# Expert blocks of a routed layer: two weight panels split whole into high and low parts, six pair places, and the gate limit moved into a product

## The reference, cut to what matters

```python
SWIGLU_LIMIT, SWIGLU_ALPHA, EXPERT_BLOCK, D_FF_3 = 7.0, 1.702, 128, 1024

def clamped_swiglu_expert(xb, w_gu, b_gu, w_dn, b_dn):      # xb: (128, 1024)
    gu = xb @ w_gu + b_gu                                   # w_gu: (1024, 2048)
    gate = jnp.minimum(gu[:, :D_FF_3], SWIGLU_LIMIT)
    up = jnp.clip(gu[:, D_FF_3:], -SWIGLU_LIMIT, SWIGLU_LIMIT)
    glu = gate * jax.nn.sigmoid(SWIGLU_ALPHA * gate)
    return ((up + 1.0) * glu) @ w_dn + b_dn                 # w_dn: (1024, 1024)

xb = hf[row_tok].reshape(NB, EXPERT_BLOCK, D)
yb = lax.map(lambda a: clamped_swiglu_expert(a[0], w_gate_up[a[1]], ...), (xb, blk_e))
```

## Time and profile before

| what | value |
|---|---|
| median of 3 runs | 3327.51 us (3325.28 to 3328.65) |
| the profiled execution | 3326.17 us, span 3324.3 us, mean granted clock 0.961 |
| TensorE busy in the span | 3106.9 us (93%) |
| VectorE busy | 1850.6 us (56%) |
| ScalarE busy | 1596.8 us (48%) |
| GpSimd busy | 738.3 us (22%) |
| DMA traffic | 694.23 MB, mean 209 GB/s |

### The profile page before, as it was taken

How to read it: one execution, slowest core, us unless ns; L and a number is a source line. 1 busy time by engine, 2 the same in 40 slices (tenths; PEclk the granted TensorE clock), 3 DMA queues, 4 the chain that set the end, 5 groups by cost and what they waited for, 6 DMA issues and landing times. The chain is left out here.

```text
span 3324.3 us, 39326 instructions
## 1 busy us (share of the span) xinstructions
PE 3106.9 (93%) x14030; PEld 2418.4 (73%) x14030; DVE 1850.6 (56%) x2260; ACT 1596.8 (48%) x2142; POOL 738.3 (22%) x381
## 2 busy tenths in 40 slices
PE   7986999998999999989998985999999999999997
PEld 6754678877877787768887774777777777777753
DVE  3257433344467404440034346888888888888764
ACT  4333434433566423242233224766766676666652
POOL 3400144442523343334442510000000000000020
PEclk9987999998999999999999977999999999999998
DMA  3243322222222132212225407999999999999971
GB/s 148 102 167 112 127 76 101 101 95 83 77 76 76 54 112 76 102 51 101 100 103 198 177 10 311 403 408 412 405 407 411 407 407 411 411 402 411 411 265 48
DMA packets 65737, 694.23 MB, mean 209 GB/s; under 512 B 6928, under 2 KB 7312, under 8 KB 25584
## 3 DMA queue, kind: packets, MB, share of 16 engines
q1 hardware_dynamic: 54480, 650.57, 49.6%
q0 software_dynamic: 7056, 25.69, 2.0%
q10 hardware_dynamic: 4112, 16.78, 1.2%
HBM read 654.74 MB, written 38.27 MB: 208 GB/s over the span
## 5 line engine op out<-in xcount | busy, mean ns | idle before, releaser
L142 POOL TENSOR_TENSOR ring_low<-ring,mix_ring_high 128x1024 fp32r<-128x1024 f32 x120 | 292.7, 2473 | 451.9 <-ACT mix_ring_high L137 451.9
L213 PE MATMUL psum<-mix_high,mix_ring_high 128*128 128x512 f32 x864 | 344.1, 398 | 13.1 <-DVE h_low L518 8.6
L215 PE MATMUL psum<-mix_high,ring_low 128*128 128x512 f32 x864 | 338.1, 391 | 0.0
L213 PE MATMUL psum<-ex_high,ex_rows_high 128*128 128x512 f32 x768 | 315.8, 411 | 7.1 <-DVE ring_low L2852 7.1
L215 PE MATMUL psum<-ex_high,ex_rows_low 128*128 128x512 f32 x768 | 300.4, 391 | 0.0
L214 PE MATMUL psum<-h_low,mix_ring_high 128*128 128x512 f32 x736 | 287.7, 391 | 0.0
L142 POOL TENSOR_TENSOR ring_low<-ring,ff_ring_high 128x1024 fp32r<-128x1024 f32 x72 | 174.9, 2463 | 417.0 <-ACT ff_ring_high L137 226.5
L2683 POOL CAST ex_index<-table 128x1 uint32 x32 | 5.9, 184 | 1069.2 <-PE psum L2701 1069.2
L2852 DVE TENSOR_TENSOR ring_low<-ring,ex_high 128x2048 fp32r<-128x2048 f32 x96 | 214.2, 2287 | 40.5 <-ACT ex_high L2794 40.5
L2852 DVE TENSOR_TENSOR ex_more_low<-ex_more,ex_high_in_x 128x2048 fp32r<-128x2048 f32 x96 | 219.5, 2287 | 20.4 <-ACT ex_high_in_x L2794 20.4
L2750 PE MATMUL psum<-ex_more,ex_act_t 128*128 128x512 f32 x512 | 224.9, 592 | 0.0
(11 more groups left out here) (586 smaller groups left out, 6915.2 us busy)
## 6 DMA issues: line engine op xcount, KB each, us to landing
ex_more<-moe_w SPq DMA_DIRECT2D x128, 2048.0 KB, 9.3
ring<-wstream SPq DMA_DIRECT2D x87, 2048.0 KB, 8.3
ring<-moe_w SPq DMA_DIRECT2D x64, 2048.0 KB, 11.2
ex_bias_up<-moe_b SPq DMA_DIRECT2D x32, 1024.0 KB, 11.2
y_rows<-ex_y SPq DMA_DIRECT2D x33, 512.0 KB, 11.2
y_rows<-mx_zero ACTq DMA_DIRECT2D x1, 16384.0 KB, 50.9
x<-xt SPq DMA_DIRECT2D x8, 256.0 KB, 5.4
rel<-rel_bias SPq DMA_DIRECT2D x1, 2048.0 KB, 9.5
```

The costliest lines, as they stand in the source:

```text
L142: e.tensor_tensor(low, full, high.bitcast(F32), ALU.subtract).then_inc(self.low_ready, 1)
L213: pe.matmul(out, a[0], b[0], start=start, stop=False)
L215: return pe.matmul(out, a[1], b[0], start=False, stop=stop)
```

## The change

- All 24 quarters are split, 12 pairs. PIECES ends with (4,2), (4,3), (5,2), (5,3). The float32 product of line 2750, `ex_act_t`, `take_act` and the semaphores `dn_done`, `a_ready` and `limited` go. TensorE ends a block with four more quarters, behind a wait for the second `low_act`.
- The ring of high quarters has 12 places; the two new ones lie in the tile h. `held_before` says which quarter must be used up before a place is written: the one 12 earlier.
- `take_gate(0)`, `take_up(0)`, `take_gate(1)` stand before pairs 6, 8 and 10; `sigmoid(0)` ahead of copy 16; `take_y` stays ahead of copy 8.
- `act_high` and `act_low` have all 8 steps; `high_act` and `low_act` run once for each half. On VectorE the tail is `low_act(0)`, `take_up(1)`, `low_rows(0)`, `low_act(1)`, `low_rows(1)`.
- `take_gate` is the bias addition alone. The limit is taken as the minimum of the silu with its value at 7 (SILU_LIMIT), in the product with up; the factor 1/1.702 moves to the copy of y.
- SP loads panels 4 and 5 after their quarter 3.

```diff
+SILU_LIMIT = SW_ALPHA * SW_LIMIT / (1.0 + float(np.exp(-SW_ALPHA * SW_LIMIT)))
...
-    RING = 10
-    PIECES = tuple((s, c) for s in range(4) for c in range(PARTS)) + tuple((s, c) for s in (4, 5) for c in range(2))
+    PAIRS = 6
+    RING = 2 * PAIRS
+    PIECES = tuple((s, c) for s in range(4) for c in range(PARTS)) + ((4, 0), (4, 1), (5, 0), (5, 1), (4, 2), (4, 3), (5, 2), (5, 3))
...
-    act_at, dve_at = (8, 14), (10, 14, 18)
+    act_at, dve_at = (8, 16), (12, 16, 20)
...
+        high_in_h = nc.alloc_sbuf_tensor_at("ex_high_in_h", [P, 2, PART], F32R, offset=g.h_at)
...
+        def held_before(n):
+
+            if n >= RING:
+                return NQ + n - RING
+            return n + RING if n + RING < NQ else n
...
-                        if s < 4:
-                            sp.wait_ge(used, b * NQ + place[s, PARTS - 1] + 1)
-                        else:
-                            sp.wait_ge(dn_done, b * 2 + s - 3)
+                        sp.wait_ge(used, b * NQ + place[s, PARTS - 1] + 1)
...
-                    pe.wait_ge(a_low, b + 1)
+                    pe.wait_ge(a_low, b * 2 + 1)
...
-                    pe.wait_ge(a_ready, b + 1)
+                    pe.wait_ge(a_low, b * 2 + 2)
                     for s in (4, 5):
-                        for k in range(4, KT):
-                            mm = pe.matmul(psum[:, s + 2, :], act_t[:, k - 4, :], weights(s, k), start=False, stop=k == KT - 1)
-                        mm.then_inc(dn_done, 1)
+                        for c in range(2, PARTS):
+                            quarter(b, s, c, psum[:, s + 2, :], act_high, act_low)
...
-                        act.activation(y[:, 512 * s:512 * s + 512], psum[:, 6 + s, :], ACT.Copy).then_inc(y_done, 1)
+                        act.wait_ge(used, b * NQ + place[4 + s, PARTS - 1] + 1)
+                        act.activation(y[:, 512 * s:512 * s + 512], psum[:, 6 + s, :], ACT.Copy, scale=1.0 / SW_ALPHA).then_inc(y_done, 1)
...
-                        act.wait_ge(used, b * NQ + n + 1 + NQ - RING)
+                        act.wait_ge(used, b * NQ + held_before(n) + 1)
...
-                    high_act(b)
+                    high_act(b, 0)
                     sigmoid(b, 1)
                     act.wait_ge(x_turned, b * 2 + 3)
                     high_rows(0)
-                    take_act(b)
+                    high_act(b, 1)
...
-                    dve.wait_ge(taken, b * 4 + 2 * c + 5)
-                    dve.tensor_scalar(gate[:, :], gate[:, :], SW_LIMIT, None, ALU.min).then_inc(limited, 1)
...
-                    dve.scalar_tensor_tensor(act_rows[:, c, :], up[:, :], 1.0 / SW_ALPHA, sig[:, :], ALU.mult, ALU.mult).then_inc(h_done, 1)
+                    dve.scalar_tensor_tensor(act_rows[:, c, :], sig[:, :], SILU_LIMIT, up[:, :], ALU.min, ALU.mult).then_inc(h_done, 1)
...
-                    low_act(b)
+                    low_act(b, 0)
                     take_up(b, 1)
-                    for c in range(2):
-                        low_rows(b * 2 + 2 + c, c)
+                    low_rows(b * 2 + 2, 0)
+                    low_act(b, 1)
+                    low_rows(b * 2 + 3, 1)
```

More of the change, by code:

```diff
@@ L2603, in expert_stage @@
         high, bias_up = r.high, r.bias_up
-        high_in_x = nc.alloc_sbuf_tensor_at("ex_high_in_x", [P, RING - 6, PART], F32R, offset=g.x_at)
+        high_in_x = nc.alloc_sbuf_tensor_at("ex_high_in_x", [P, 4, PART], F32R, offset=g.x_at)
+        high_in_h = nc.alloc_sbuf_tensor_at("ex_high_in_h", [P, 2, PART], F32R, offset=g.h_at)
         rows_high, _ = on_line(nc, own, "ex_rows_high", [P, DT, P], F32R)
         rows_low = sb("rows_low", [P, DT, P], F32R)
-        act_high, act_low, act_t = sb("act_high", [P, 4, P], F32R), sb("act_low", [P, 4, P], F32R), sb("act_t", [P, 4, P])
+        act_high, act_low = sb("act_high", [P, KT, P], F32R), sb("act_low", [P, KT, P], F32R)
         part_of = lambda c: slice(c * PART, (c + 1) * PART)
@@ L2611, in expert_stage @@
         weights = lambda s, k: piece(s)[:, k * PANEL:(k + 1) * PANEL]
+        def held_before(n):
+            if n >= RING:
+                return NQ + n - RING
+            return n + RING if n + RING < NQ else n
         def slots(n, count):
             n %= RING
-            at = high[:, n:n + count, :] if n < 6 else high_in_x[:, n - 6:n - 6 + count, :]
+            tile, n = (high, n) if n < 6 else (high_in_x, n - 6) if n < 10 else (high_in_h, n - 10)
+            at = tile[:, n:n + count, :]
             return at.rearrange("p a f -> p (a f)")
@@ L2622, in expert_stage @@
         y = sb("y", [P, D])
-        used, high_ready, low_ready, dn_done = (sem(n) for n in ("used", "high_ready", "low_ready", "dn_done"))
+        used, high_ready, low_ready = (sem(n) for n in ("used", "high_ready", "low_ready"))
         x_turned, x_high, x_low, up_in = (sem(n) for n in ("x_turned", "x_high", "x_low", "up_in"))
-        taken, limited, sig_ready, product, h_done, h_turned, a_high, a_low, a_ready, y_done, y_out = (sem(n) for n in (
-            "taken", "limited", "sig_ready", "product", "h_done", "h_turned", "a_high", "a_low", "a_ready", "y_done", "y_out"))
+        taken, sig_ready, product, h_done, h_turned, a_high, a_low, y_done, y_out = (sem(n) for n in (
+            "taken", "sig_ready", "product", "h_done", "h_turned", "a_high", "a_low", "y_done", "y_out"))
         passed, table_set = (sem(n) for n in ("passed", "table_set"))
@@ L2696, in _ @@
                 pe.sem_inc(used, NQ)
-                pe.sem_inc(dn_done, 2)
                 def turn_rows(c):
@@ L2759, in high_rows, with high_act @@
                         .then_inc(x_high, 1)
[L2761 to L2767, removed]
+                def high_act(b, c):
+                    act.wait_ge(h_turned, b * 2 + c + 1)
+                    act.activation(act_high[:, 4 * c:4 * c + 4, :].rearrange("p k s -> p (k s)"), psum[:, 4, :], ACT.Copy).then_inc(a_high, 1)
                 def take_y(b):
@@ L2771, in take_y @@
                     for s in range(2):
-                        act.wait_ge(dn_done, b * 2 + s + 1)
-                        act.activation(y[:, 512 * s:512 * s + 512], psum[:, 6 + s, :], ACT.Copy).then_inc(y_done, 1)
+                        act.wait_ge(used, b * NQ + place[4 + s, PARTS - 1] + 1)
+                        act.activation(y[:, 512 * s:512 * s + 512], psum[:, 6 + s, :], ACT.Copy, scale=1.0 / SW_ALPHA).then_inc(y_done, 1)
                 def sigmoid(b, c):
-                    act.wait_ge(limited, b * 2 + c + 1)
+                    act.wait_ge(taken, b * 4 + 2 * c + 5)
                     act.wait_ge(h_done, b * 2 + c + 2)
@@ L2813, in low_rows, with low_act @@
                         .then_inc(x_low, 1)
[L2815 to L2818, removed]
+                def low_act(b, c):
+                    part = slice(4 * c, 4 * c + 4)
+                    dve.wait_ge(a_high, b * 2 + c + 1)
+                    dve.tensor_tensor(act_low[:, part, :].rearrange("p k s -> p (k s)"), psum[:, 4, :],
+                                      act_high[:, part, :].rearrange("p k s -> p (k s)").bitcast(F32), ALU.subtract)\
                         .then_inc(a_low, 1)
@@ L3224, in build @@
         g.sums, g.sums_at = placed(nc, ctx, "sums", [P, 3, S], F32)
+        g.h_at = -(-nc.sbuf_base // 32) * 32
         h, g.h_low = with_low(nc, ctx, "h", [P, DT, S])
```

## The result

| kernel | median (runs) | ratio to before, 95% interval |
|---|---|---|
| before | 3328.08 us | |
| changed | 3380.69 us (3379.75 to 3382.17) | 1.0158 (1.0146 to 1.0170) |

The change costs 52.6 us; 3351 us, +23, was forecast, in a range of 3340 to 3370, and the time lies above it. The profiled execution of the changed kernel took 3379.75 us (span 3377.9 us).

The account below looks back on a forecast made before the run. TensorE was taken as the bound at 35.96 us a block; after the change a loop through three engines, 36.68 us. Later `low_act(0)` (+26.4) less 2.5 won back gave +23.9 us: 3351 us, range 3340 to 3370.

Parts of the forecast that it names:

- What bounds the kernel before: Expert stage: TensorE, busy 300 of 300 us, sets the 35.96 us block; the DMA queue is close behind.
- Part 1: TensorE: split products replace the plain float32 product, saving 1.42 us a block; TensorE alone would give 34.54 us.
- Parts 2 and 3: VectorE gets 3.49 us more before `low_act(0)`; the loop through VectorE, TensorE and ScalarE goes from 33.19 to 36.68 us a block.
- the restart of TensorE: Between `low_act(0)` and quarter (4,0): 0.06 us after the subtraction's 0.68, together 0.74 us of the loop.
- the piece from (4,0) to `turn_act(1)`: TensorE's part of the three-engine loop, taken as 2.86 us in each block.
- rival (c): TensorE's idle 2.1 us a block drops its clock: +1.4 to +2.86 us a block, 3395 to 3440 us; 6%.
- Rival (a): The three-engine loop is shorter than reckoned, so TensorE or the DMA queue binds: about 3302 us, between 3281 and 3325; 9%.
- (b): The DMA queue holds the block at 35.96 us if the loop does not: no change, 3322 to 3333 us; 4%.
- (d): A supply wait besides, copy 9 or panel s5 late: +0.2 to +0.5 us a block, 3358 to 3368 us; 6%.
- the margin at pair 4: ScalarE's copy 9 ends at 3.1 us, VectorE's pair 4 wants it at 3.4: 0.3 us to spare.

Follow-up runs that it names:

- the kernel with the tail moved: Changed kernel with `low_act(0)`, `take_up(1)` and `low_rows(0)` put before pair 11 on VectorE instead of behind it: 3283.45 us, ratio 0.9869.
- The filled kernel: Changed kernel with 7 more matmuls, product overwritten, between `turn_rows(0)` and TensorE's wait for `low_act(0)`: 3352.91 us, ratio 1.0070.
- the kernel with the small bias load: Changed kernel with `low_act(0)`, `take_up(1)`, `low_rows(0)` before pair 11, and the bias load cut to 64 of 2048 columns: 3282.41 us, ratio 0.9865.

## Why the prediction was wrong

- **What bounds the kernel before: right.** VectorE's 0.92 us taken away there changes nothing, and TensorE's saving shows in full once no loop is in its way.
- **Part 1, TensorE at 34.54 us: right,** 34.54 measured in the kernel with the tail moved.
- **Parts 2 and 3, the loop at 36.68 us: right,** 36.73 in all blocks at full clock. The filled kernel, in which the clock stays up, has 3352.9 us against the forecast 3351. The only piece off by more than 0.02 us is the restart of TensorE, 0.82 for 0.74.
- **Where it failed: the sum took the piece from (4,0) to `turn_act(1)` at full clock in every block, 2.86 us, and the clock's falls at nothing.** In 17 of 31 blocks that piece took about 4.4 us, 27 us more in all. This is rival (c), which was given 6% and left out of the range. Its place and mechanism were right (TensorE's idle time before (4,0), then that piece at the lower clock) and its price per fall too (1.59 us, forecast 1.4 to 2.86). Its reach was not: I priced it as in every block or in none, 3395 to 3440, and the measured time lies between the forecast and that. The evidence that I weighed it by was one row, 2.66 us idle before 1140.16 with the clock at 1.00. One such gap shows that the clock can stay up after it, not that it will: in the changed kernel the same gap of 1.97 us, 31 times, had both outcomes. A fall in every second block was a case of its own, 3351 + 16 x 1.59 = 3376, and the range should have held it; the measured time is 4 us above that, of which 1.6 are the seventeenth fall and 1.5 the loop's.
- The Trainium skill, "TensorE: Matmul & The Clock Gate" (HAM oscillation), describes a loop in which a wait for a DMA, longer than the wait here, brought the clock down in every single pass. The changed kernel agrees that a wait in a loop can bring the clock down again and again, but not in every pass: 17 falls in 31 spacings.
- **Rival (a) did not come, and its floor was wrong too.** I took the best slice of the kernel before, 421 GB/s, as what the queue can do, so 34.8 us. The kernel with the moved tail carries 425 GB/s at 34.54 us and is not held by it: a rate seen while TensorE sets the demand is no ceiling. "DMA: Bandwidth & Descriptors" in the Trainium skill (Specifications) gives 435 GB/s as the ceiling of the fabric, and the 425 over 600 us stay under it (a stretch of 3.3 us above has 437). It also gives about 358 GB/s as the limit of HBM for a core, half of what two cores share; here, with one core at work, even the kernel with the small bias load has 396.
- Rivals (b) and (d) did not come: the margin at pair 4 held (no wait of VectorE inside the pairs), and ScalarE waited for 0.2 us of landings in all from 2100 to 3150 us.

## What to carry to other kernels

Before an engine at 100% is given less to do, walk the loops that run from one pass to the next through the other engines, and compare each with the pass: here a loop with 2.8 us to spare got 3.5 us more, and busy shares of 83% and 68% did not show it. When a wait will recur on TensorE in every pass, price falls of the clock in a part of the passes, too: here 1.97 us of idle time brought them in half of the blocks and 1.74 us in none, and one row with the clock up after a gap said nothing on that. A few matmuls in the idle time are a cheap test of what the clock costs. If the loop goes through an engine's fixed order, try the order before giving the work back: what others wait for goes ahead of what is needed later, and when one loop is cut, look for the one behind it.

## What the hardware showed that was not expected

- The falls of the clock have a pattern. In the changed kernel they come 75.1 us apart for most of the stage, which is one short and one long block (36.73 + 38.31 = 75.04), and each lasts 3.41 us. Behind 2.88 us of idle time the clock fell in 21 of 31 blocks; behind 1.97 us in 16 of 31; behind 1.74 us, 1.27 and 0.35 us in none. (The first block is left out: its idle time is longer, 3.91, 2.62, 2.50, 1.74 and 1.26 us, and the clock fell behind the first three.) Each count is from one profiled execution. In each of these kernels the idle time recurs at the same place of a block, behind 35 to 36 us of dense matmuls. What decides between two equal gaps was not tested; that the falls come so regularly speaks against chance.
- The DMA engines carried 425 GB/s over 600 us with TensorE busy for all of the time and at full clock beside them.
